# Three passes on split halves for two products of the second block, and square roots by ScalarE from PSUM

## The chip, the cores and the metric

The kernel runs on one core of a Trainium2 chip. The metric is the device time of one execution in microseconds. TensorE (PE) multiplies, VectorE (DVE) and ScalarE (ACT) do elementwise work, GpSimd (POOL) a little, and SyncE (SP) issues nearly all transfers.

## The reference, cut to what matters

A network of three blocks on 256 tokens of width 1024, in fp32. The change lies in the second block, a mixer with two branches. Cut to the lines that matter:

```
h = rmsnorm(x) @ w_in
lru_x, lru_gate, q, k, v, qi, ki, wi, gate_a, gate_b = split(h)
ua = conv(lru_x)
r, i = sigmoid(ua @ wa + ba), sigmoid(ua @ wx + bx)      # blocks of 128
ya = (lru_scan(r, i, ua) * gelu(lru_gate)) @ w_lru_br
qh, kh = rmsnorm(q per head), rmsnorm(k per head)         # q * rsqrt(mean(q*q) + EPS) * q_norm
yb = attention(qh, kh, v, top-k by qi, ki, wi) @ w_attn_br
merged = sigmoid(gate_a) * ya + sigmoid(gate_b) * yb
x = x + merged @ w_out
```

The feed-forward part of the second block follows at once, then the third block.

## The kernel before

Every engine has its own program, written out by hand in the order in which the stages run; semaphores order them against each other. There is no planner: the order in the code is the order of each queue. `make_plan` only counts. It numbers the batches of products (`products_done`), gives each batch of kind "W" one of four work banks in rotation (`bank[4]` to `bank[7]`), and each weight slab one of `NSLOT` = 3 ring slots. `open_bank` makes PE wait until the batch four "W" earlier in the rotation has been read (`bank_copied`). SP loads slab n as soon as the last batch that reads slab n - 3 is done; a slab is 2 MB in two transfers of 1 MB.

A product of activations and weights comes in two forms. The plain one (`feature_major`, `to_acc`) takes the fp32 tiles as they are, one matmul for each 128 rows of the contraction; the trace shows each such matmul as two records. The split one (`feature_major3`, `to_acc3`, both by way of `mm3`) writes each factor as a high half, rounded to fp32r, and a low half, the rest, and makes three matmuls: high by high, high by low, low by high. For this ACT copies a slab's high half into a split area (`high`, two pieces of 128x2048), and DVE subtracts it to get the low half (`low`, two pieces); PE waits for `low_ready`.

The stages of the second block that the prediction speaks of, in PE's order:

- `qk_ms`: five products with `ones_mean` (L1256) give the mean squares of q and k, 128x512 each. DVE adds `EPS` (L2542), which frees the bank, and takes the reciprocal (L2544) in `msq`, two buffers in turn; ACT takes the square root (`rsq`, L1848); DVE multiplies it onto q or k (L2546).
- `qi`: a split product, 96 matmuls on two work banks.
- `lru_ri`: eight batches of plain matmuls (L1265), copied out by ACT with a sigmoid (L1853). On ACT the square roots of `qk_ms` stand between the copies of `qi` and these sigmoids.
- `kiwi`, `gate_a`, the indexer with `gate_b`, `logits2`, `lru_out`: plain products. Beside them DVE runs the LRU's scan, the top-k and the softmax.
- `pv2`: for four pairs of heads m, six transposes (L1321 to L1323) into two banks, ACT's two copies to `pT2`, then four matmuls with v (L1333, L1334) and ACT's copy to `o2`.
- `attn_out` (two slabs, 64 plain matmuls, L954), then on DVE a product with a gate and a sum into `merged` for each of its four batches (L2640, L2645); `w_out2` (two slabs, 32 plain matmuls of 512 columns, L1002) adds to the accumulators.
- `norm3` (L922) and the feed-forward, in split form from the start.

```
        for m in range(4):
            for d in range(2):
                b = open_bank("pv2", 3 * m + d)
                batch(causal_blocks(b, lambda t: att[t][:, 2 * m + d, :]))
...
        all_copied("pv2", (2, 5, 8, 11))
        for s in range(2):
            feature_major("attn_out", 2 * s, s, o2, DC)
        pe.wait_ge(S["merged_ready"], 4)
        for s in range(2):
            to_acc("w_out2", s, merged)
```

Of the kernel before, what the change touches and what calls it, by code (L numbers as in the profile page):

```python
# [31 lines left out]
T, D = 256, 1024  # L32
# [168 lines left out]
def make_plan():  # L201
# [94 lines left out]
def network(nc, dram, out, const_at, col_at, row_at):  # L296
# [189 lines left out]
    xn_flat = xn[:, :, :].rearrange("p t d -> p (t d)")  # L486
    w_o_areas = [[AB[:, 0:2048], AB[:, 2048:4096]] if len(split_areas(f"w_o{h}", 0)) == 1 else [xn_flat, A[8][:, :]]
                 for h in range(2)]
# [111 lines left out]
    def wide(a, dim, n):  # L600
# [8 lines left out]
             "xn_ready", "conv_ready", "z_ready", "logit_ready", "exp_ready", "prob_ready", "mask_ready",  # L609
             "zeroed", "msq_ready", "sel_ready", "sel_prob_ready", "xe_ready", "w_scaled", "slots_ready", "e_y_ready", "rows_out", "bias_in",  # L610
             "lam_exp_in", "lam_exp_out", "sp_ready", "ua_ready", "tanh_done", "decay_done", "mult_in",
             "mult_out", "scan_done", "lru_ready", "rsq_ready", "qk_ready", "relu_used", "att_in", "att_exp",
             "att_ready", "merged_ready", "conv_in", "gelu_done", "rope_ready", "final_row_in", "high_ready",
             "low_ready", "high_norm", "h0_split", "y_high", "o_high", "hid_whole", "hid_split", "cmp_x_ready", "cmp_in",
# [5 lines left out]
             "ffnorm2", "swa_norm", "ffnorm3", "final"]  # L620
    N_INPUTS, N_FILLS = 16 * 9, 5
    R_NORMS = [2, 4, 6, 7, 8, 9, 10, 11]
# [234 lines left out]
    def _(pe):  # L857
# [138 lines left out]

        def to_acc(name, s, src):

            w = slab(name, s)
            for t in range(TT):  # L1000
                for k in range(DC):
                    last = mm(acc[t][s][:, :], src[:, k, t * P:(t + 1) * P], w[:, 512 * k:512 * k + 512],  # L1002
                              start=(k == 0), stop=(k == DC - 1))
            batch(last)

        pe.wait_ge(fills_done, N_FILLS)
# [312 lines left out]
        def causal_blocks(b, p_of_t):  # L1319
# [3 lines left out]
            return nc.tensor.transpose(b[:, 2 * P:3 * P], p_of_t(1)[:, P:2 * P], ident)  # L1323

        for m in range(4):
            for d in range(2):
                b = open_bank("pv2", 3 * m + d)
                batch(causal_blocks(b, lambda t: att[t][:, 2 * m + d, :]))
            b = open_bank("pv2", 3 * m + 2)
            g = m // 2  # L1330
            for d in range(2):
                copied(pe, "pv2", 3 * m + d)
                mm(b[:, d * T:(d + 1) * T], v2[:, 0, g * P:(g + 1) * P], pT2[d][:, 0:T], start=True, stop=False)  # L1333
                last = mm(b[:, d * T + P:(d + 1) * T], v2[:, 1, g * P:(g + 1) * P], pT2[d][:, T:T + P],  # L1334
                          start=False, stop=True)
# [325 lines left out]
    def _(act):  # L1661
# [38 lines left out]
        def high(name, s, it=0):  # L1700

            j = split_number(name, s) - 1
            if plan.times[name] == 1 and j >= 2 and not name.startswith("ffn"):
# [152 lines left out]
        for i in range(2):  # L1856
            rsq(2 * i)
            if i == 0:
                rsq(1)
            copy_out("qi", i, qi[:, 2 * i:2 * i + 2, :].rearrange("p g t -> p (g t)"))  # L1860
        ri(0)
        rsq(3)
        for i in range(1, 5):
            ri(i)
        rsq(4)
        for i in range(5, 8):
            ri(i)
# [34 lines left out]
        for t in range(TT):  # L1902
# [4 lines left out]
            ins.then_inc(S["att_exp"], 1)  # L1907
        for m in range(4):
            for d in range(2):
                copy_out("pv2", 3 * m + d, pT2[d][:, 0:384], n=384)  # L1910
            copy_out("pv2", 3 * m + 2, o2[:, 2 * m:2 * m + 2, :].rearrange("p g t -> p (g t)"))
        filled(act, "attn_out", 3)
# [176 lines left out]
    def _(pool):  # L2089
        pool.dma_start(cols[:, :], dram("cols")).then_inc(cols_loaded, 16)  # L2090
        fills = [(c_pad[:, :, :], 0.0), (ones[:, :], 1.0), (ones_mean[:, :], 1.0 / P), (zeros[:, :], 0.0),
                 (neg_half[:, :], -0.5)]
        assert len(fills) == N_FILLS
# [48 lines left out]
    def _(dve):  # L2142
# [396 lines left out]
        for i in range(5):  # L2539
            a, r = (q2[:, 2 * i:2 * i + 2, :] if i < 4 else k2[:, :, :]).rearrange("p c t -> p (c t)"), msq[i % 2]  # L2540
# [93 lines left out]
        for i in range(1, 4):  # L2634
            gated_lru(i)
        for i in range(4):
            copied(dve, "gate_b", GATE_B_AT[i])
# [5 lines left out]
            copied(dve, "lru_out", i)  # L2643
            a = merged[:, two, :].rearrange("p c t -> p (c t)")
            v.tensor_tensor(a, a, tmp[i % 2][:, :], ALU.add).then_inc(S["merged_ready"], 1)  # L2645
        low("ffn2_first", 0)
# [359 lines left out]
```

## Time and profile before

| | |
|---|---|
| time before, median of 3 runs | 2821.01 us (2817.1 to 2821.4) |
| the profiled execution's own time | 2818.57 us |
| its span | 2816.7 us |
| PE busy | 2463.9 us, 87% of the span |
| DVE busy | 1266.4 us, 45% |
| ACT busy | 776.6 us, 28% |
| `qk_ms` to `kiwi` on PE | 1314.7 to 1350.0 us |
| `pv2` to the end of `w_out2` on PE | 1453.9 to 1522.8 us |

The profile is one execution. Each engine's share is an average over the whole program; what a stage is limited by is read in its own stretch of time. "Idle before" beside an instruction says how long its engine had nothing to do, and which instruction let it go on. PEclk is the granted clock of TensorE as a share of 2.4 GHz; 0.50 is the lower of its two levels, 1.2 GHz. A matmul's listed duration includes its pipeline; the pace of a stream of matmuls is the distance of their starts.

### The profile page before, as it was taken

The numbers are of one execution on the slowest core, as the hardware profiler recorded it, in microseconds if no ns is written. First come the engines' busy times: TensorE is split into PE (matmuls) and PEld (weight loads), VectorE is DVE, ScalarE is ACT, GpSimd is POOL, SyncE is SP. The second block draws the span as 40 slices with busy tenths as digits, with TensorE's granted clock in tenths as the row PEclk, the third lists the DMA queues.
The fourth block names the chain that finished last, engine by engine and source line by source line (L and its number), as shares of the span: only waits on it lengthen the run. The fifth ranks groups of instructions, "written<-read, shape, count | busy, mean of one in ns | idle before, by whom it ended". The sixth has DMA issues, their size and how long they took to land.

```text
span 2816.7 us, 35438 instructions
## 1 busy us (share of the span) xinstructions
PE 2463.9 (87%) x14525; PEld 1712.4 (61%) x14526; DVE 1266.4 (45%) x1841; ACT 776.6 (28%) x1102; POOL 22.3 (1%) x39
## 2 busy tenths in 40 slices
PE   6999877677677766789999999999989999997998
PEld 4997222121122212158787998888958888885887
DVE  2365100000000000046544776876576778776676
ACT  3342000000000000034422334434264434345432
POOL 1000000000000000000000000000000000000000
PEclk9999876777776777799999999999999999998999
DMA  8667999999999999984434554554404555551553
GB/s 319 227 238 305 407 416 416 418 418 419 418 417 417 418 419 418 418 310 139 152 120 150 183 193 170 178 187 166 152 27 150 179 181 192 183 175 61 180 179 120
DMA packets 272134, 720.74 MB, mean 256 GB/s; under 512 B 11240, under 2 KB 129016, under 8 KB 238880
## 3 DMA queue, kind: packets, MB, share of 16 engines
q1 hardware_dynamic: 270000, 708.88, 66.5%
q0 software_dynamic: 2032, 10.40, 1.0%
q8 instruction: 76, 1.25, 0.2%
q14 instruction: 26, 0.21, 0.0%
HBM read 718.17 MB, written 3.16 MB: 256 GB/s over the span
## 4 chain that ended last, share of the span: by engine, by line
PE 52%; issue 41%; DVE 3%; DMA 2%; ACT 2%; POOL 0%; SPq 0%; DVEq 0%; POOLq 0%; ACTq 0%
PE bank L1363 9%; PE bank L887 6%; PE bank L888 6%; PE bank L889 6%; PE bank L1364 4%; PE bank L954 4%; PE bank_pair L887 4%; PE bank_pair L888 3%; PE bank_pair L889 3%; DVE ring_r L2169 1%; PE bank_pair L1002 1%; DMA ring<-in_w_in 1%; PE bank L1014 1%; DVE HT L2797 0%; PE bank_pair L1529 0%
## 5 line engine op out<-in xcount | busy, mean ns | idle before, releaser
L1364 PE MATMUL bank<-HT_r,ring_r 128*128 128x256 f32 x1408 | 395.1, 281 | 0.0
L2428 DVE TENSOR_TENSOR A<-bank,A 128x512 f32<-128x512 f32 x16 | 11.1, 691 | 582.3 <-PE bank L1163 582.3
L1364 PEld LDWEIGHTS bank<-HT_r,ring_r 128*128 128x128 f32 x1408 | 266.2, 189 | 0.7
L889 PE MATMUL bank<-HT_r,ring_r 128*128 128x256 f32 x904 | 255.7, 283 | 0.0
L1363 PE MATMUL bank<-HT_r,AB_r 128*128 128x512 f32 x640 | 228.4, 400 | 1.5 <-DVE HT_r L2177 1.5
L1363 PE MATMUL bank<-HT_r,AC_r 128*128 128x512 f32 x640 | 226.5, 398 | 0.0
L2169 DVE TENSOR_TENSOR ring_r<-ring,AB_r 128x2048 fp32r<-128x2048 f32 (+1 forms) x80 | 177.5, 2260 | 101.2 <-ACT AB_r L1707 101.2
L1163 PE MATMUL bank<-ring,A 128*32 128x512 f32 x768 | 141.3, 825 | 77.6 <-DMA ring<-in_w_gate_e 43.4
L2169 DVE TENSOR_TENSOR ring_r<-ring,A_r 128x2048 fp32r<-128x2048 f32 (+1 forms) x89 | 191.8, 2190 | 21.8 <-ACT A_r L1707 21.8
L2169 DVE TENSOR_TENSOR ring_r<-ring,AC_r 128x2048 fp32r<-128x2048 f32 x66 | 148.5, 2289 | 74.9 <-ACT AC_r L1707 74.7
L889 PE MATMUL bank_pair<-A_r 128*128 128x512 f32 x456 | 178.7, 392 | 0.0
L1707 ACT ACTIVATE AB_r<-ring 128x2048 fp32r<-128x2048 f32 (+1 forms) x80 | 146.7, 1883 | 108.2 <-DMA ring<-in_w_up 36.5
L888 PE MATMUL bank_pair<-ring_r,A_r 128*128 128x512 f32 x448 | 174.5, 390 | 0.0
L889 PEld LDWEIGHTS bank<-HT_r,ring_r 128*128 128x128 f32 x904 | 173.4, 192 | 0.0
L1919 ACT ACTIVATE tmp<-tmp 128x256 f32<-128x256 f32 x112 | 46.8, 418 | 436.4 <-DVE tmp L2690 321.0
L1707 ACT ACTIVATE A_r<-ring 128x2048 fp32r<-128x2048 f32 (+1 forms) x89 | 158.9, 1827 | 3.2 <-PE bank L954 3.2
L1667 ACT ACTIVATE A<-bank 128x256 f32<-128x256 f32 (+1 forms) x69 | 30.1, 447 | 450.9 <-PE bank L1170 302.3
L887 PE MATMUL bank_pair<-A_r 128*128 128x512 f32 x384 | 149.7, 390 | 0.0
L2210 DVE TENSOR_REDUCE tmp<-bank 128x256 f32<-128x512 f32 x176 | 120.7, 686 | 63.3 <-PE bank L1364 63.2
L1707 ACT ACTIVATE AC_r<-ring 128x2048 fp32r<-128x2048 f32 x66 | 123.2, 1916 | 88.2 <-DMA ring<-in_ffn_w_gu 78.1
L1795 ACT ACTIVATE A<-bank 128x512 f32<-128x512 f32 x16 | 9.6, 597 | 497.8 <-PE bank L1163 497.8
L1363 PEld LDWEIGHTS bank<-HT_r,AB_r 128*128 128x128 f32 x640 | 120.6, 189 | 31.4 <-issue 2.1
(502 smaller groups left out, 4614.9 us busy)
## 6 DMA issues: line engine op xcount, KB each, us to landing
ring<-in_ffn_w_gu SPq DMA_DIRECT2D x88, 1024.0 KB, 7.5
ring<-in_w_up_e SPq DMA_DIRECT2D x48, 1024.0 KB, 26.6
ring<-in_w_gate_e SPq DMA_DIRECT2D x48, 1024.0 KB, 22.8
ring<-in_w_down_e SPq DMA_DIRECT2D x48, 1024.0 KB, 19.5
ring<-in_w_in SPq DMA_DIRECT2D x46, 1024.0 KB, 7.3
ring<-in_ffn_w_down SPq DMA_DIRECT2D x40, 1024.0 KB, 6.5
A<-in_w_gate_e SPq DMA_DIRECT2D x32, 1024.0 KB, 19.0
A<-in_w_up_e SPq DMA_DIRECT2D x32, 1024.0 KB, 26.7
```

Source lines behind the costliest of these rows:

```text
L887: mm(out_, lhs[0], rhs[0], start=start, stop=False, skip_group_check=True)
L888: mm(out_, lhs[0], rhs[1], start=False, stop=False, skip_group_check=True)
L889: return mm(out_, lhs[1], rhs[0], start=False, stop=stop, skip_group_check=True)
L954: last = mm(b[:, f * T:(f + 1) * T], w[:, at:at + P], src[:, k, :], start=(k == 0), stop=(k == n_k - 1))
L1163: last = mm(b[32 * j:32 * j + 32, :], xe_now[:, k, :], w[:, 512 * j:512 * j + 512], start=(k == 0), stop=(k == DC - 1), tile_position=(0, ...
L1363: mm(both, high, h_both[:, :, k, :], start=(k == 0), stop=False, skip_group_check=True)
L1364: last = mm(both[:, 1, :], low, h_high[:, k, :], start=False, stop=(k == DC - 1), skip_group_check=True)
L1667: frees(run(dst, work_bank(name, i)[0:rows_, 0:n], ACT.Copy, scale=scale), name, i)
L1707: run(area[:, :], w[:, at:at + area.shape[1]], ACT.Copy).then_inc(S["high_ready"], 1)
L1919: run(f_act[b % 2], f_conv[b % 2], fn).then_inc(S["gelu_done"], 1)
L2169: v.tensor_tensor(twins[f"ring{slot}"][:, part], ring[slot][:, part], area[:, :].bitcast(fp32), ALU.subtract).then_inc(S["low_ready"], 1)
L2210: frees(v.tensor_reduce(dst, both, AX.X, ALU.add), name, i)
```

## The change

In the `qk_ms` stage ACT reads the mean squares straight from PSUM, adds `EPS` as the activation's bias (a new column `eps_col`, filled by POOL at the start) and writes the root to one of five buffers `root` (four in `xn`, one in `tmp[2]`); DVE takes the reciprocal there. All five roots stand ahead of the copies of `qi` on ACT.

`attn_out` and `w_out2` become split products. Their slabs are split by ACT and DVE (`high`, `low`), `o2` and `merged` are written as high and low halves, PE turns the next pair of heads in `pv2` before it multiplies the present one (`pT2` has four buffers now), and it starts `w_out2` without waiting for all four parts of `merged`.

```diff
+def pv2_at(m, part, d=0):
+    if part == "out":
+        return 3 * m + 4 if m < 3 else 11
+    return d if m == 0 else 3 * m - 1 + d
...
-    p.add("attn_out", "WWWW", [1, 3])
-    p.add("w_out2", "AA", [0, 1])
+    p.add("attn_out", "WWWW", [1, 3], split=2)
+    p.add("w_out2", "AA", [0, 1], split=2)
...
-        for m in range(4):
+        pv2_turned(0)
         for m in range(4):
-            for d in range(2):
-                b = open_bank("pv2", 3 * m + d)
-                batch(causal_blocks(b, lambda t: att[t][:, 2 * m + d, :]))
-            b = open_bank("pv2", 3 * m + 2)
+            if m < 3:
+                pv2_turned(m + 1)
+            b = open_bank("pv2", pv2_at(m, "out"))
...
-        all_copied("pv2", (2, 5, 8, 11))
+        def o2_fresh(k):
+            if k % 2 == 0:
+                copied(pe, "pv2", pv2_at(k // 2, "out"))
+            return o2_parts(k)
         for s in range(2):
-            feature_major("attn_out", 2 * s, s, o2, DC)
-        pe.wait_ge(S["merged_ready"], 4)
-        for s in range(2):
-            to_acc("w_out2", s, merged)
+            feature_major3("attn_out", 2 * s, s, o2_parts if s else o2_fresh, src=o2_parts)
+        def pair_merged(k):
+            if k % 2 == 0:
+                pe.wait_ge(S["merged_ready"], k // 2 + 1)
+        to_acc3("w_out2", 0, merged_high, merged_low, ready=pair_merged)
+        to_acc3("w_out2", 1, merged_high, merged_low)
...
# ScalarE
-        def rsq(i):
-            act.wait_ge(S["msq_ready"], i + 1)
-            run(msq[i % 2][:, :], msq[i % 2][:, :], ACT.Sqrt).then_inc(S["rsq_ready"], 1)
+        for i in range(5):
+            filled(act, "qk_ms", i)
+            frees(run(root[i][:, :], work_bank("qk_ms", i)[:, :], ACT.Sqrt, bias=eps_col[:, 0:1]), "qk_ms", i)
...
+        copied(act, "logits2", 7)
+        for s in range(2):
+            high("attn_out", s)
+        for m in range(5):
+            if m < 4:
+                for d in range(2):
+                    copy_out("pv2", pv2_at(m, "turned", d), pT2[2 * (m % 2) + d][:, 0:384], n=384)
+            if m:
+                two_ = slice(2 * m - 2, 2 * m)
+                filled(act, "pv2", pv2_at(m - 1, "out"))
+                run(o2_high[:, two_, :].rearrange("p g t -> p (g t)"),
+                    work_bank("pv2", pv2_at(m - 1, "out"))[:, :], ACT.Copy).then_inc(S["o2_high"], 1)
+        for s in range(2):
+            high("w_out2", s)
...
# VectorE
-            filled(dve, "qk_ms", i)
-            frees(v.tensor_scalar(r[:, :], work_bank("qk_ms", i)[:, :], EPS, None, ALU.add), "qk_ms", i)
             copied(dve, "qk_ms", i)
-            v.reciprocal(r[:, :], r[:, :]).then_inc(S["msq_ready"], 1)
-            dve.wait_ge(S["rsq_ready"], i + 1)
+            link(v.reciprocal(r[:, :], r[:, :]))
...
         for i in range(1, 4):
             gated_lru(i)
+            if i < 3:
+                low("attn_out", i - 1)
+        for m in range(4):
+            i, two = pv2_at(m, "out"), slice(2 * m, 2 * m + 2)
+            dve.wait_ge(S["o2_high"], m + 1)
+            frees(v.tensor_tensor(o2_low[:, two, :].rearrange("p g t -> p (g t)"), work_bank("pv2", i)[:, :],
+                                  o2_high[:, two, :].rearrange("p g t -> p (g t)").bitcast(fp32), ALU.subtract),
+                  "pv2", i)
+        low("w_out2", 0)
...
-            v.tensor_tensor(a, a, tmp[i % 2][:, :], ALU.add).then_inc(S["merged_ready"], 1)
+            v.tensor_tensor(a_high, a, tmp[i % 2][:, :], ALU.add)
+            v.tensor_tensor(a, a, tmp[i % 2][:, :], ALU.add).then_inc(S["merged_whole"], 1)
+            dve.wait_ge(S["merged_whole"], i + 1)
+            v.tensor_tensor(a_low, a, a_high.bitcast(fp32), ALU.subtract).then_inc(S["merged_ready"], 1)
+        low("w_out2", 1)
         low("ffn2_first", 0)
```

ScalarE's queue from the copy of v to the sigmoids of `lru_ri`, before (L1667 copies a batch of `qi`; L1848 is the root, L1853 the sigmoid; the first row is the copy of v):

```order
L1667 ACTIVATE A<-bank 128x512
L1848 ACT_TABLE_LOAD
L1848 ACTIVATE tmp<-tmp 128x512 x2
L1667 ACTIVATE A<-bank 128x512
L1848 ACTIVATE tmp<-tmp 128x512
L1667 ACTIVATE A<-bank 128x512
L1853 ACT_TABLE_LOAD
L1853 ACTIVATE AC<-bank,cols 128x256 x2
L1848 ACT_TABLE_LOAD
L1848 ACTIVATE tmp<-tmp 128x512
L1853 ACT_TABLE_LOAD
L1853 ACTIVATE AC<-bank,cols 128x256 x6
```

The same place on ScalarE in the changed kernel (L1873 is the root, L1692 the copy, L1878 the sigmoid):

```order
L1692 ACTIVATE A<-bank 128x512
L1873 ACT_TABLE_LOAD
L1873 ACTIVATE xn<-bank,eps_col 128x512 x4
L1873 ACTIVATE tmp<-bank,eps_col 128x512
L1692 ACTIVATE A<-bank 128x512 x2
L1878 ACT_TABLE_LOAD
L1878 ACTIVATE AC<-bank,cols 128x256 x8
L1878 ACTIVATE A<-bank,cols 128x256 x8
```

The five roots now read the banks and stand in one row under one table load; the sigmoids are no longer interrupted.

TensorE's queue in `pv2`, before (L1321 to L1323 transpose a head, L1333 and L1334 multiply with v; `tmp2`, `tmp3` hold the turned heads):

```order
L1321 MATMUL bank7<-consts,A4 128x128
L1322 MATMUL bank7<-consts,A8 128x128
L1323 MATMUL bank7<-consts,A8 128x128
L1333 MATMUL bank4<-tmp2,A5 128x256
L1334 MATMUL bank4<-tmp2,A5 128x128
L1333 MATMUL bank4<-tmp3,A5 128x256
L1334 MATMUL bank4<-tmp3,A5 128x128
L1321 MATMUL bank5<-consts,A4 128x128
```

The same place on TensorE in the changed kernel (L1327 to L1329 transpose, L1346 and L1347 multiply):

```order
L1327 MATMUL bank7<-consts,A4 128x128
L1328 MATMUL bank7<-consts,A8 128x128
L1329 MATMUL bank7<-consts,A8 128x128
L1327 MATMUL bank4<-consts,A4 128x128
L1328 MATMUL bank4<-consts,A8 128x128
L1329 MATMUL bank4<-consts,A8 128x128
L1327 MATMUL bank5<-consts,A4 128x128
L1328 MATMUL bank5<-consts,A8 128x128
L1329 MATMUL bank5<-consts,A8 128x128
L1346 MATMUL bank6<-tmp2,A5 128x256
L1347 MATMUL bank6<-tmp2,A5 128x128
```

The six transposes of the next pair now stand between a pair's transposes and its product.

VectorE's queue from the second gated part of `lru_out` (L2649) to the first split of `w_out2` in the changed kernel (L2196 is `low`, L2666 the low half of `o2`); before, only the three rows of L2649 (there L2624) stood here, without the others:

```order
L2649 TENSOR_TENSOR A<-bank,AC 128x512
L2196 TENSOR_TENSOR ring_r<-ring,AB_r 128x2048 x2
L2649 TENSOR_TENSOR A<-bank,AC 128x512
L2196 TENSOR_TENSOR ring_r<-ring,xn_r 128x2048
L2196 TENSOR_TENSOR ring_r<-ring,HT_r 128x2048
L2649 TENSOR_TENSOR A<-bank,AC 128x512
L2666 TENSOR_TENSOR HT_r<-bank,AC_r 128x512 x4
L2196 TENSOR_TENSOR ring_r<-ring,A_r 128x2048 x2
```

The splitting of both slabs of `attn_out` stands between the gated parts of `lru_out`.

## Rows read from the trace of the kernel before

**Rows 1.** The page: the chain that ended last, by engine.
```profile
PE 52%; issue 41%; DVE 3%; DMA 2%; ACT 2%; POOL 0%; SPq 0%; DVEq 0%; POOLq 0%; ACTq 0%
```

**Rows 2.** Stretches: length, busy of PE, PEld, DVE, ACT, POOL, PEclk, DMA.
```profile
1322.00:1326.00 4.00, 3.99 (x21) 4.00 (x22) 3.30 (x2) 0.63 (x1) 0.00 (x0) 0.57 0.00 0
1454.00:1466.00 12.00, 9.14 (x58) 7.74 (x57) 0.69 (x1) 5.55 (x12) 0.00 (x0) 1.00 0.49 175
```

**Rows 3.** Timeline of PE from `qk_ms` to `kiwi`.
```profile
1318.11 1.02 PE L1256 MATMUL bank<-tmp,ones_mean 128*128 128x512 f32 x2
1322.01 0.36 PE L887 MATMUL bank<-AB_r,AC_r 128*128 128x256 f32 x1 [2.88 <-DVE tmp L2542]
...
1325.13 0.41 PE L887 MATMUL bank<-AB_r,A_r 128*128 128x256 f32 x1
...
1328.01 0.28 PE L888 MATMUL bank<-AB_r,A_r 128*128 128x256 f32 x1
1328.13 0.28 PE L889 MATMUL bank<-AB_r,ring_r 128*128 128x256 f32 x1
...
1335.09 1.03 PE L1265 MATMUL bank<-AC,ring 128*128 128x256 f32 x4
1341.42 8.64 PE L1265 MATMUL bank<-AC,ring 128*128 128x256 f32 x28 [5.30 <-DVE tmp L2542]
1349.99 6.31 PE L1270 MATMUL bank<-HT,w_kiwi 128*64 128x256 f32 x32
```

**Rows 4.** Timeline of ACT, then of DVE, in and behind that stretch.
```profile
1315.49 1.28 ACT L1848 ACT_TABLE_LOAD   x1
...
1337.20 0.84 ACT L1853 ACTIVATE AC<-bank,cols 128x256 f32<-128x256 f32 x2
...
1321.90 3.35 DVE L2544 RECIPROCAL tmp<-tmp 128x512 f32<-128x512 f32 x1
...
1390.40 0.28 DVE L2577 TENSOR_SCALAR A<-A,small 128x128 f32<-128x128 f32 x1 [5.30 <-ACT A L1894]
```

**Rows 5.** Timeline from `pv2` to `w_out2`.
```profile
1453.92 0.27 PE L1321 MATMUL bank<-consts,A 128*128 128x128 f32 x1
...
1454.47 0.27 PE L1323 MATMUL bank<-consts,A 128*128 128x128 f32 x1
...
1455.09 0.67 PE L1333 MATMUL bank<-tmp,A 128*128 128x256 f32 x2 [0.34 <-ACT tmp L1667]
...
1456.47 0.27 PE L1321 MATMUL bank<-consts,A 128*128 128x128 f32 x1
...
1465.75 27.86 PE L954 MATMUL bank<-AC,ring 128*128 128x256 f32 x128 [0.99 <-ACT AC L1667]
...
1495.19 27.73 PE L1002 MATMUL bank_pair<-ring,A 128*128 128x512 f32 x64 [1.58 <-DVE A L2645]
```

**Rows 6.** Timeline of PE in `swa_out`, a split product of the third block.
```profile
2595.18 0.77 PE L887 MATMUL bank_pair<-A_r,HT_r 128*128 128x512 f32 x1 [4.59 <-DVE A_r L2893]
...
2597.87 0.63 PE L887 MATMUL bank_pair<-A_r,HT_r 128*128 128x512 f32 x1
2598.30 0.63 PE L888 MATMUL bank_pair<-ring_r,HT_r 128*128 128x512 f32 x1
...
2599.03 0.39 PE L887 MATMUL bank_pair<-A_r,HT_r 128*128 128x512 f32 x1
...
2601.79 0.39 PE L887 MATMUL bank_pair<-A_r,HT_r 128*128 128x512 f32 x1
```

**Rows 7.** Splitting a slab on ACT and DVE; a slab's issue and landing.
```profile
1501.91 3.71 ACT L1707 ACTIVATE AB_r<-ring 128x2048 fp32r<-128x2048 f32 x2 [36.52 <-DMA ring<-in_w_up]
1503.85 4.49 DVE L2169 TENSOR_TENSOR ring_r<-ring,AB_r 128x2048 fp32r<-128x2048 f32 x2 [8.71 <-ACT AB_r L1707]
...
1440.31 0.92 SPq L698 DMA_DIRECT2D ring<-in_w_attn_br  x2
...
ring<-in_w_attn_br SPq DMA_DIRECT2D x2, 1024.0 KB, 6.1
```

More of the change, by code:

```diff
@@ L350, in network @@
     neg_half = sb("neg_half", [P, 2 * TT])
+    eps_col = sb("eps_col", [P, 1])
     tmp = [sb(f"tmp{i}", [P, 512]) for i in range(4)]
@@ L468, in split_areas @@
             return [(0, t_["A3"]), (2048, twins["xn"][:, :, :].rearrange("p t d -> p (t d)"))]
+        if name == "attn_out":
+            xn_r = twins["xn"][:, :, :].rearrange("p t d -> p (t d)")
+            return [(0, t_["AB"])] if s == 0 else [(0, xn_r), (2048, twins["HT"][:, 2048:4096])]
+        if name == "w_out2":
+            a, b = (("A4", "A8"), ("A5", "A6"))[s]
+            return [(0, t_[a]), (2048, t_[b])]
         if name == "swa_kv":
@@ L486, in network @@
     xn_flat = xn[:, :, :].rearrange("p t d -> p (t d)")
+    root = [xn_flat[:, 512 * i:512 * i + 512] for i in range(4)] + [tmp[2]]
     w_o_areas = [[AB[:, 0:2048], AB[:, 2048:4096]] if len(split_areas(f"w_o{h}", 0)) == 1 else [xn_flat, A[8][:, :]]
@@ L995, in to_acc3 @@
             batch(last)
[L997 to L1004, printed above, removed]
         pe.wait_ge(fills_done, N_FILLS)
@@ L1323, in causal_blocks, with pv2_turned, o2_parts @@
             return nc.tensor.transpose(b[:, 2 * P:3 * P], p_of_t(1)[:, P:2 * P], ident)
+        def pv2_turned(m):
+            for d in range(2):
+                b = open_bank("pv2", pv2_at(m, "turned", d))
+                batch(causal_blocks(b, lambda t: att[t][:, 2 * m + d, :]))
+        pv2_turned(0)
         for m in range(4):
-            for d in range(2):
-                b = open_bank("pv2", 3 * m + d)
-                batch(causal_blocks(b, lambda t: att[t][:, 2 * m + d, :]))
-            b = open_bank("pv2", 3 * m + 2)
+            if m < 3:
+                pv2_turned(m + 1)
+            b = open_bank("pv2", pv2_at(m, "out"))
             g = m // 2
             for d in range(2):
-                copied(pe, "pv2", 3 * m + d)
-                mm(b[:, d * T:(d + 1) * T], v2[:, 0, g * P:(g + 1) * P], pT2[d][:, 0:T], start=True, stop=False)
-                last = mm(b[:, d * T + P:(d + 1) * T], v2[:, 1, g * P:(g + 1) * P], pT2[d][:, T:T + P],
+                copied(pe, "pv2", pv2_at(m, "turned", d))
+                p = pT2[2 * (m % 2) + d]
+                mm(b[:, d * T:(d + 1) * T], v2[:, 0, g * P:(g + 1) * P], p[:, 0:T], start=True, stop=False)
+                last = mm(b[:, d * T + P:(d + 1) * T], v2[:, 1, g * P:(g + 1) * P], p[:, T:T + P],
                           start=False, stop=True)
             batch(last)
-        all_copied("pv2", (2, 5, 8, 11))
-        for s in range(2):
-            feature_major("attn_out", 2 * s, s, o2, DC)
-        pe.wait_ge(S["merged_ready"], 4)
-        for s in range(2):
-            to_acc("w_out2", s, merged)
+        def o2_parts(k):
+            return o2_high[:, k, :], o2_low[:, k, :]
+        def o2_fresh(k):
+            if k % 2 == 0:
+                copied(pe, "pv2", pv2_at(k // 2, "out"))
+            return o2_parts(k)
+        for s in range(2):
+            feature_major3("attn_out", 2 * s, s, o2_parts if s else o2_fresh, src=o2_parts)
[4 more added lines that the diff above has]
+        to_acc3("w_out2", 1, merged_high, merged_low)
         def gate_up_tile(name, i, w, j, it=0, parts=h_parts):
@@ L1702, in high @@
             j = split_number(name, s) - 1
-            if plan.times[name] == 1 and j >= 2 and not name.startswith("ffn"):
+            if plan.times[name] == 1 and j >= 2 and not name.startswith("ffn") \
+                    and name not in ("attn_out", "w_out2"):
                 act.wait_ge(products_done, plan.split_end[j - 2])
@@ L1856, in _ @@
         for i in range(2):
-            rsq(2 * i)
-            if i == 0:
-                rsq(1)
             copy_out("qi", i, qi[:, 2 * i:2 * i + 2, :].rearrange("p g t -> p (g t)"))
[L1861 to L1866, printed above, removed]
+        for i in range(8):
             ri(i)
@@ L1907, in _ @@
             ins.then_inc(S["att_exp"], 1)
-        for m in range(4):
-            for d in range(2):
-                copy_out("pv2", 3 * m + d, pT2[d][:, 0:384], n=384)
-            copy_out("pv2", 3 * m + 2, o2[:, 2 * m:2 * m + 2, :].rearrange("p g t -> p (g t)"))
+        copied(act, "logits2", 7)
[3 more added lines that the diff above has]
+            if m < 4:
+                for d in range(2):
+                    copy_out("pv2", pv2_at(m, "turned", d), pT2[2 * (m % 2) + d][:, 0:384], n=384)
[6 more added lines that the diff above has]
+            high("w_out2", s)
         filled(act, "attn_out", 3)
@@ L2539, in _ @@
         for i in range(5):
-            a, r = (q2[:, 2 * i:2 * i + 2, :] if i < 4 else k2[:, :, :]).rearrange("p c t -> p (c t)"), msq[i % 2]
-            filled(dve, "qk_ms", i)
-            frees(v.tensor_scalar(r[:, :], work_bank("qk_ms", i)[:, :], EPS, None, ALU.add), "qk_ms", i)
+            a = (q2[:, 2 * i:2 * i + 2, :] if i < 4 else k2[:, :, :]).rearrange("p c t -> p (c t)")
+            r = root[i]
             copied(dve, "qk_ms", i)
-            v.reciprocal(r[:, :], r[:, :]).then_inc(S["msq_ready"], 1)
-            dve.wait_ge(S["rsq_ready"], i + 1)
+            link(v.reciprocal(r[:, :], r[:, :]))
             v.scalar_tensor_tensor(a, a, col("q_norm_2" if i < 4 else "k_norm_2"), r[:, :], ALU.mult, ALU.mult)\
@@ L2643, in _ @@
             copied(dve, "lru_out", i)
-            a = merged[:, two, :].rearrange("p c t -> p (c t)")
-            v.tensor_tensor(a, a, tmp[i % 2][:, :], ALU.add).then_inc(S["merged_ready"], 1)
+            a, a_high, a_low = (m_[:, two, :].rearrange("p c t -> p (c t)")
+                                for m_ in (merged, merged_high, merged_low))
+            v.tensor_tensor(a_high, a, tmp[i % 2][:, :], ALU.add)
[3 more added lines that the diff above has]
+        low("w_out2", 1)
         low("ffn2_first", 0)
```

16 lines of the change are left out of this document (8 added, 8 removed).

## The prediction

> **What bounds the kernel now.** I read the page's chain first: PE holds 52% of it and PE's own issue 41%, DVE, DMA and ACT 7% together [rows 1]. The expert stage apart, where transfers limit, the program is as long as PE's stream of matmuls plus the holes in it. So I looked for holes around the two places that the change touches, in the timeline of PE.
>
> In the first place there are two. PE finishes the last mean square at 1319.1 (1318.11 + 1.02) and starts `qi` at 1322.01, after 2.88 us of idle time; it does one batch of `lru_ri` at 1335.09 and sits idle for 5.30 us until 1341.42. Both rows name DVE's L2542, which frees a bank that the next batch needs [rows 3]. DVE frees one bank per round of add, reciprocal (3.35 us), ACT's root and product [rows 4]. The clock shows too: PEclk is 0.57 from 1322 to 1326 [rows 2], and the matmuls there start 0.208 us apart (1322.01 to 1325.13, fifteen matmuls), against 0.12 later [rows 3].
>
> In the second place, `pv2` goes in rounds: six transposes, a wait for ACT's copy, four matmuls with v, a wait for the next. Only 9.14 of 12 us are busy, with PEclk 1.00 [rows 2]. Then `attn_out` takes 27.86 us for 128 records (64 matmuls), 1.58 us pass until `merged` is whole, and `w_out2` takes 27.73 us for 64 records (32 matmuls) [rows 5]. These two run without a hole: there the matmuls themselves are the limit.
>
> **The change part by part.** The sum is made against the profiled execution's own 2818.57 us, 2.4 below the median of 2821.01. Times below are on the clock of the trace before.
>
> *Roots.* ACT's table load ends at 1316.77 [rows 4]. A root of 128x512 from PSUM is not in the trace before; I take it as some 0.6 us, since two sigmoids of half the size take 0.84 [rows 4]; even at 0.84 nothing changes below. The bank of the second mean square, which `qi` needs first, is then free at about 1318, before PE is through the fifth product at 1319.1. `qi` starts at 1319.1, not 1322.01. Its 96 matmuls need 96 x 0.12 = 11.5 us and end at 1330.6, not 1335.09: 4.5 us gained, 2.9 of it idle time and 1.6 low clock.
>
> `lru_ri` is 4 + 28 = 32 records [rows 3]. At the pace of `attn_out`, 27.86 / 128 = 0.218 us [rows 5], they take 7.0 us. The stage ends at 1337.6, where `kiwi` starts; before, `kiwi` started at 1349.99 [rows 3]. Is ACT fast enough? It copies the last batch of `qi` after 1330.6 (0.6 us), loads a table (1.28), then needs 0.86 per batch [rows 4]: the first is done near 1333.4, when PE, four banks ahead, asks for it at 1334.1. It keeps step. **Gain 12.4 us** (1349.99 - 1337.6). If `lru_ri` still ran at low clock as it did in part before (28 records in 8.64 us, 2.5 more than at 0.218), it is 9.9.
>
> DVE must come as much earlier, or PE meets it later. Its five rounds lose the add and the wait for the root, and end near 1338; its next work waits for ACT's last sigmoid, near 1339.5. Before, that sigmoid could not end before the last batch of `lru_ri`, at 1350.0. So DVE goes on at least 10.5 us earlier, against PE's 12.4, and it was idle for 5.30 us before the first score [rows 4], which covers the rest. The stages from `kiwi` to `lru_out` move as a whole.
>
> *pv2.* A transpose is 0.11 us (1453.92 to 1454.47, five steps), a round's product 1.38 (1455.09 to 1456.47) [rows 5]. With the next pair's transposes ahead of the product, ACT's copies lie beside them. 24 x 0.11 + 4 x 1.38 = 8.2 us instead of 11.83 (1453.92 to 1465.75): **3.6 us gained**. The bank of a turned pair is freed by ACT's copy one round earlier, that of a product by DVE's low half. The last low half comes some 1.9 us after the last product; `attn_out` needs it only at its seventh k, 6 x 0.36 = 2.2 us in. That cover is thin; without it it costs tenths.
>
> *attn_out.* 64 plain matmuls become 192 split ones at 0.12 us [rows 3], the same 256 columns: 23.0 instead of 27.86 us, **4.8 gained**.
>
> *Between.* DVE now makes four passes of 0.7 us for the last part of `merged`, 2.9 us. But `w_out2` starts with parts 0 to 2 and meets part 3 after 6 x 0.69 = 4.1 us. **1.5 us gained** (the 1.58). If this cover failed, about as much is lost again.
>
> *w_out2.* 32 matmuls become 96. In `swa_out` the same shape starts every 0.23 us (2599.03 to 2601.79, twelve) [rows 6]: 22.1 instead of 27.73, **5.6 gained**.
>
> Here a rule can be set beside the rows, outside of the sum. The Trainium skill (FP8 and Floating Point Precision, TensorE Precision Notes) says that true FP32 takes four passes through the array. By its page TensorE: Matmul & The Clock Gate (Back-to-back issue gap) a pass takes N / 2.4 + 2.5 ns, 109 ns for 256 columns and 216 for 512. The plain pace here (0.218 for one of two records) agrees with four such passes. The split pace (0.12 and 0.23) is slower than the rule. By the rule the two products would take 20.9 and 20.7 us, 3.5 less than my sum. No run here shows it; the rows decide.
>
> *Splitting.* A slab costs ACT 3.71 and DVE 4.49 us, DVE starting 1.94 behind ACT [rows 7]; four new slabs. For `attn_out`'s second slab the transfers are issued at 1440.31 and land after 6.1 us, so near 1447.3; ACT splits until 1451.0, DVE until 1453.8, just before the first transposes end. Behind ACT's splitting stand the copies of `pv2`, wanted at 1454.4: 3.4 us to spare. Behind DVE's stands the last gated part of `lru_out`, which frees the bank for the fourth turned head: a few tenths to spare. `w_out2`'s first slab is split while `attn_out` runs. Its second is loaded when `attn_out`'s first slab is used up (1473.6), split by ACT until about 1485, by DVE behind the last part of `merged`, 1488 to 1492.5. PE wants it when the first half of `w_out2` ends, near 1496. `ffn2_first`'s first slab is issued when `attn_out` ends, as before, and wanted a full `w_out2` later. All of this costs nothing while these covers hold. The one more fill on POOL at the start lies under the first transfers.
>
> Sum: 12.4 + 3.6 + 4.8 + 1.5 + 5.6 = 27.9 us. 2818.57 - 27.9 = 2790.7; I say 2791.
>
> **The rivals.**
> (a) *The splitting comes late.* DVE or ACT is behind at one of the thin places, PE waits some microseconds and falls to the low clock. `swa_out` shows the pattern: 4.59 us idle for a low half, then matmuls 0.43 apart until 2598.7 (eight, 1.6 us lost) [rows 6]. One such wait costs 6.2 us: 2797. Against it: the slack above.
> (b) *The hole of the roots is met again.* If DVE's chain to the scores did not come forward, PE would get its 12.4 us but hand back all beyond DVE's 5.30 us of slack, 7.1: 2798. Against it: DVE's own earlier start.
> (c) *A split matmul takes half a plain record.* A plain record of 256 columns starts every 0.218 us, one of 512 every 27.73 / 64 = 0.433 [rows 5]. If each is two passes and a split matmul one, 192 x 0.109 + 96 x 0.217 = 41.8 us stand against my 45.1, 3.3 less: 2787. Against it: split matmuls start 0.12 and 0.23 us apart [rows 3, 6]. The rule of four passes, in the Trainium skill (FP8 and Floating Point Precision, TensorE Precision Notes), would make it so.
> (d) *Slower than before.* The split products run at low clock throughout. Then they start 0.208 and 0.43 us apart: 192 x 0.208 + 96 x 0.43 = 81.2 us instead of 45.1, and the time is 2827. It decides once 77% of them (27.9 of 36.1) run low. For it: PE falls after every long hole. Against it: PEclk is 1.00 even in `pv2` with its holes [rows 2].
> (e) *The change does not do what it says*, the roots or the products wait for something not seen, and nothing is gained: 2819.
>
> **How the numbers follow.** The full sum 0.72, (a) 0.13, (b) 0.05, (c) 0.04, (d) 0.03, (e) 0.03. The likeliest case has a range of its own of 2787 to 2795: `pv2` between its sum and 1 us more, the low clock in `lru_ri` 2.5 more, a slack that fails by tenths. To leave out no more than 2 in 10 I take (c) in and (a) and (b) nearly: 2786 to 2799. Faster by over 0.2% (5.6 us, about what a measurement tells from no change) hold all but (d) and (e): 0.94; same 0.03; slower 0.03.
>
> **What would show it.** Right: no idle time of PE over 1 us from the mean squares to `kiwi`, `kiwi` 12 us earlier, one table load for the roots and one for the sigmoids; 192 matmuls in 23 us and 96 in 22; the first `norm3` transpose 28 us earlier. Wrong: an idle row of PE in `pv2`, at the start of `attn_out` or between the halves of `w_out2` with DVE's or ACT's splitting as its releaser, PEclk under 0.9 from `pv2` to `w_out2`, or a longer wait for the scores.

## The result, and the profile after

| | before | changed |
|---|---|---|
| median of 4 runs each | 2821.19 us (2817.1 to 2821.4) | 2790.85 us (2787.4 to 2793.43) |
| ratio, with its 95% interval | | 0.9895 (0.9878 to 0.9912) |
| the profiled execution's span | 2816.7 us | 2791.6 us |

The kernel became faster by 30.3 us, 1.05%; the interval of the ratio leaves out 1. A second set of runs of the two gave 2818.07 and 2789.74 us, ratio 0.9902 (0.9885 to 0.9918). The prediction was 2791, with a range of 2786 to 2799.

The page's chain of the changed kernel reads as before, answering to [rows 1]: the program is still PE's stream and its issue.

```profile
PE 53%; issue 41%; DVE 3%; ACT 1%; DMA 1%; POOL 0%; DVEq 0%; SPq 0%; POOLq 0%; ACTq 0%
```

The timeline of PE in the changed kernel, from the first mean square to `gate_a`, answers to [rows 3] (L1262 the mean squares, L902 to L904 the split matmuls, L1271 `lru_ri`, L1276 and L1282 the two batches of `kiwi`, L969 plain matmuls):

```profile
1317.42 3.59 PE L1262 MATMUL bank<-A,ones_mean 128*128 128x512 f32 x8
1320.85 1.02 PE L1262 MATMUL bank<-tmp,ones_mean 128*128 128x512 f32 x2
1321.31 0.68 PE L902 MATMUL bank<-AB_r,AC_r 128*128 128x256 f32 x1
...
1333.22 7.07 PE L1271 MATMUL bank<-AC,ring 128*128 128x256 f32 x32
1340.22 6.32 PE L1276 MATMUL bank<-HT,w_kiwi 128*64 128x256 f32 x32
1346.47 4.65 PE L1282 MATMUL bank<-w_kiwi,HT 128*128 128x8 f32 x32
1350.97 1.63 PE L969 MATMUL bank<-HT,ring 128*128 128x256 f32 x3
```

No row has idle time any more. `qi` follows the last mean square, and the 32 records of `lru_ri` run as one group of 7.07 us. ACT's rows show why, beside [rows 4]: one table load, four roots within 2.42 us, the fifth 0.69.

```profile
1318.23 1.28 ACT L1873 ACT_TABLE_LOAD   x1
1319.53 2.42 ACT L1873 ACTIVATE xn<-bank,eps_col 128x512 f32<-128x512 f32 x4
1321.91 0.69 ACT L1873 ACTIVATE tmp<-bank,eps_col 128x512 f32<-128x512 f32 x1
```

The timeline from `pv2` to the feed-forward in the changed kernel answers to [rows 5]:

```profile
1445.81 0.27 PE L1327 MATMUL bank<-consts,A 128*128 128x128 f32 x1
...
1446.69 0.27 PE L1329 MATMUL bank<-consts,A 128*128 128x128 f32 x1
1447.09 0.33 PE L1327 MATMUL bank<-consts,A 128*128 128x128 f32 x1
...
1453.95 0.36 PE L902 MATMUL bank<-AC_r,AB_r 128*128 128x256 f32 x1
...
1477.07 0.40 PE L902 MATMUL bank_pair<-A_r,AC_r 128*128 128x512 f32 x1
...
1498.86 2.20 PE L937 MATMUL bank<-consts,x 128*128 128x128 f32 x16
1501.57 0.36 PE L902 MATMUL bank<-HT_r,AB_r 128*128 128x256 f32 x1 [0.50 <-DVE HT_r L2204]
```

`pv2` takes 8.14 us (1445.81 to 1453.95), `attn_out` 23.12, `w_out2` 21.79, and nothing lies between them. The starts from 1446.69 to 1447.09 are 0.40 us apart where transposes otherwise start every 0.11: a small hole of 0.3 us. Over both products PE is busy throughout and PEclk is 1.00 (length, PE busy, PEclk, share and rate of the transfers):

```profile
1454.00:1498.00 44.00, 44.00 (x287) 1.00 0.44 144
```

To compare kernels I take stretches of PE's timeline, from the start of one stage's first matmul to the next's, since these hardly vary, while the time at which the first mean square starts does (1313.3 to 1317.6 us over the profiles of this study, whose code up to there is nearly the same: the expert stage, bound by transfers, varies).

| stretch, us | before | changed | roots_only | products_only |
|---|---|---|---|---|
| first mean square to `kiwi` | 35.31 | 22.80 | 22.80 | 35.26 |
| second batch of `kiwi` to the indexer | 33.08 | 34.74 | 34.74 | 33.08 |
| `pv2` | 11.83 | 8.14 | 11.83 | 8.04 |
| `attn_out`, with the gap behind it | 29.44 | 23.12 | 29.44 | 23.12 |
| `w_out2` | 27.58 | 21.79 | 27.58 | 21.79 |
| first mean square to the feed-forward | 210.79 | 184.15 | 199.94 | 194.85 |

The stretches that the table leaves out, up to the feed-forward, are the same in all four within 0.01 us: `kiwi`'s first batch 6.25, the indexer to `pv2` 64.6, `norm3` 2.70.

The profiled spans differ by 25.1 us. The stretches of the last line differ by 26.64. The changed execution came 2.74 us later to the first mean square (1317.42 against 1314.68), and its part behind the feed-forward's start was 1.20 us shorter (1290.03 against 1291.23). Both lie outside of the changed code.

### The profile page after: what moved, and what is told of

It reads as the page before. It is cut to its first block, busy times and chain, and to the rows that moved or that the text cites. A ratio compares the mean times of both kernels' runs of the same rounds, so it can differ in the third digit from the quotient of the medians.

```text
span 2791.6 us, 35652 instructions
## 1 busy us (share of the span) xinstructions
PE 2459.9 (88%) x14622; PEld 1722.5 (62%) x14622; DVE 1289.0 (46%) x1856; ACT 785.5 (28%) x1106; POOL 22.4 (1%) x40
## 3 DMA queue, kind: packets, MB, share of 16 engines
q8 instruction: 76, 1.25, 0.2%
## 4 chain that ended last, share of the span: by engine, by line
PE 53%; issue 41%; DVE 3%; ACT 1%; DMA 1%; POOL 0%; DVEq 0%; SPq 0%; POOLq 0%; ACTq 0%
PE bank L1388 9%; PE bank L902 6%; PE bank L903 6%; PE bank L904 6%; PE bank L1389 4%; PE bank_pair L902 4%; PE bank_pair L903 4%; PE bank_pair L904 4%; PE bank L969 3%; DVE ring_r L2196 1%; PE bank L1020 1%; DVE HT L2836 0%; PE bank L1492 0%; PE bank L1508 0%; DVE small L2824 0%
## 5 line engine op out<-in xcount | busy, mean ns | idle before, releaser
L904 PE MATMUL bank<-HT_r,ring_r 128*128 128x256 f32 x904 | 256.1, 283 | 0.0
L2196 DVE TENSOR_TENSOR ring_r<-ring,AB_r 128x2048 fp32r<-128x2048 f32 (+1 forms) x82 | 182.0, 2261 | 96.5 <-ACT AB_r L1733 96.5
L1169 PE MATMUL bank<-ring,A 128*32 128x512 f32 x768 | 147.1, 857 | 77.0 <-DMA ring<-in_w_gate_e 42.7
L2196 DVE TENSOR_TENSOR ring_r<-ring,A_r 128x2048 fp32r<-128x2048 f32 (+1 forms) x93 | 200.8, 2194 | 22.8 <-ACT A_r L1733 22.8
L904 PE MATMUL bank_pair<-A_r 128*128 128x512 f32 x488 | 191.6, 393 | 0.0
L2196 DVE TENSOR_TENSOR ring_r<-ring,AC_r 128x2048 fp32r<-128x2048 f32 x66 | 148.5, 2289 | 72.7 <-ACT AC_r L1733 72.6
L904 PEld LDWEIGHTS bank<-HT_r,ring_r 128*128 128x128 f32 x904 | 173.8, 192 | 0.0
L1733 ACT ACTIVATE A_r<-ring 128x2048 fp32r<-128x2048 f32 (+1 forms) x93 | 166.4, 1830 | 19.5 <-DMA ring<-in_w_out 16.3
L1692 ACT ACTIVATE A<-bank 128x256 f32<-128x256 f32 (+1 forms) x69 | 30.4, 450 | 458.7 <-PE bank L1176 303.6
L902 PE MATMUL bank_pair<-A_r 128*128 128x512 f32 x384 | 149.7, 390 | 0.0
L903 PE MATMUL bank<-HT_r,AB_r 128*128 128x256 f32 x504 | 143.0, 284 | 0.0
## 6 DMA issues: line engine op xcount, KB each, us to landing
ring<-in_w_up_e SPq DMA_DIRECT2D x48, 1024.0 KB, 26.6
A<-in_w_up_e SPq DMA_DIRECT2D x32, 1024.0 KB, 26.6
```

The costliest lines, as they stand in the source:

```text
L902: mm(out_, lhs[0], rhs[0], start=start, stop=False, skip_group_check=True)
L903: mm(out_, lhs[0], rhs[1], start=False, stop=False, skip_group_check=True)
L904: return mm(out_, lhs[1], rhs[0], start=False, stop=stop, skip_group_check=True)
L1169: last = mm(b[32 * j:32 * j + 32, :], xe_now[:, k, :], w[:, 512 * j:512 * j + 512], start=(k == 0), stop=(k == DC - 1), tile_position=(0, ...
L1692: frees(run(dst, work_bank(name, i)[0:rows_, 0:n], ACT.Copy, scale=scale), name, i)
L2196: v.tensor_tensor(twins[f"ring{slot}"][:, part], ring[slot][:, part], area[:, :].bitcast(fp32), ALU.subtract).then_inc(S["low_ready"], 1)
```

## The experiments

**roots_only** is the kernel before with the roots' part alone.

```diff
+        for i in range(5):
+            filled(act, "qk_ms", i)
+            frees(run(root[i][:, :], work_bank("qk_ms", i)[:, :], ACT.Sqrt, bias=eps_col[:, 0:1]), "qk_ms", i)
...
-            frees(v.tensor_scalar(r[:, :], work_bank("qk_ms", i)[:, :], EPS, None, ALU.add), "qk_ms", i)
```

> The kernel before with the roots' part alone. Theory (two separate gains): from the first mean square to kiwi 22.8 us, as in the changed kernel (22.80), against 35.31 before; from pv2 to norm3 68.9 us as before; time 12 us (less what is handed back behind kiwi, about 1.7) under the kernel before, so 0.9955 to 0.9965 of it. Rival (the parts help each other, the roots alone only move the wait): the stretch shortens, but PE waits later, at the scores or at lru_out, and the time falls by 7 us or less.

Measured: 2805.9 us against 2819.44, ratio 0.9950 (0.9934 to 0.9967). The stretch is 22.80 us, the rest as in the table: 10.85 us gained up to the feed-forward. The stretches came as the theory says and the rival is out; the time fell by 13.5 us, a little more than forecast, and the interval reaches into the forecast. The 1.66 us handed back behind `kiwi` appear here too, without the split products. The roots' part changes several things at once: ACT frees the bank in its first step, the roots have five buffers instead of two, and they stand ahead of the copies of `qi` under one table load. Which of them counts was not tested.

**products_only** is the changed kernel with the roots made as before.

```diff
+            rsq(2 * i)
+            if i == 0:
+                rsq(1)
             copy_out("qi", i, qi[:, 2 * i:2 * i + 2, :].rearrange("p g t -> p (g t)"))
```

> The changed kernel with the roots made as before (DVE adds, ACT roots a copy). Theory: first mean square to kiwi 35.3 us as before; pv2 to norm3 53.1 us as in the changed kernel (53.05, before 68.85); time about 16 us under the kernel before, 0.994 to 0.995 of it. Rival (the splitting on ACT and DVE only fits because the roots' part moved DVE forward): PE waits in pv2 or attn_out and the stretch is 55 us or more.

Measured: 2801.8 us against 2819.44, ratio 0.9937 (0.9920 to 0.9953), again a little more than forecast. From `pv2` to `norm3` 52.95 us, with no idle row. The splitting fits without the roots' part. By stretches the two parts alone give 10.85 + 15.94 = 26.79 us, together 26.64: they add up.

The next four kernels (merged_wait, dve_late, pv2_rounds, four_passes) ran once each, with 2793.91, 2792.55, 2793.31 and 2805.01 us. A single time moves by several us with the expert stage, so only their stretches are read.

**merged_wait** takes the cover away that hides the last part of `merged`.

```diff
+        pe.wait_ge(S["merged_ready"], 4)
         to_acc3("w_out2", 0, merged_high, merged_low, ready=pair_merged)
```

> The changed kernel, but PE waits for all four parts of merged before it starts w_out2. Theory (the cover of 4.1 us hides DVE's four passes of 0.7 us): PE idle for 2.9 to 3.1 us between attn_out and w_out2, then matmuls 0.43 us apart for 2 to 4 us, so that w_out2's stretch grows by 1 to 2 us as well: attn_out's end to norm3 26 to 27 us instead of 21.8. Rival (DVE's last part is done at once, the gap before was only the semaphores' way): 22 to 23.5 us.

The timeline of PE in merged_wait, at the start of `w_out2`:

```profile
1477.67 0.50 PE L902 MATMUL bank_pair<-A_r,AC_r 128*128 128x512 f32 x1 [2.91 <-DVE A_r L2684]
1478.00 0.39 PE L903 MATMUL bank_pair<-ring_r,AC_r 128*128 128x512 f32 x1
...
1479.49 0.63 PE L902 MATMUL bank_pair<-A_r,AC_r 128*128 128x512 f32 x1
1479.91 0.63 PE L903 MATMUL bank_pair<-ring_r,AC_r 128*128 128x512 f32 x1
```

PE waits 2.91 us, and a little later the starts are 0.42 us apart. The stretch from `attn_out` to `w_out2` is 26.19 us (3.07 more), `w_out2` itself 23.49 (1.70 more): together from the end of `attn_out` to `norm3` 26.6 us, as the theory says. Waiting part by part is worth 4.77 us here, and over a third of it is the clock (PEclk is 0.50 from 1479 to 1482).

**dve_late** gives DVE 4.6 us more work ahead of the last gated part of `lru_out`.

```diff
+            if i == 3:
+                for _ in range(2):
+                    link(v.tensor_tensor(A[6][:, :], A[6][:, :], A[6][:, :], ALU.max))
             gated_lru(i)
```

> The changed kernel with two passes of DVE over 128x2048 (2.3 us each, results used by nothing) ahead of the last gated part of lru_out. Theory (DVE's cover there is used up, the changed kernel's PE already waits 0.3 us for that bank): PE waits 4.6 us more in pv2, after which the clock falls for some 3 to 4 us; pv2 8.1 to 13 us, and attn_out's start runs at the low clock if the fall outlasts pv2: pv2 to the end of attn_out 31.3 to 36.5-38 us. Rival (PE has slack there that the trace does not show): under 33 us.

The timeline of dve_late in `pv2`, DVE and PE:

```profile
1442.09 4.61 DVE L2662 TENSOR_TENSOR A<-A 128x2048 f32<-128x2048 f32 x2
...
1446.74 0.69 DVE L2649 TENSOR_TENSOR A<-bank,AC 128x512 f32<-128x512 f32 x1
...
1447.49 0.47 PE L1327 MATMUL bank<-consts,A 128*128 128x128 f32 x1 [4.64 <-DVE A L2649]
1447.76 0.42 PE L1328 MATMUL bank<-consts,A 128*128 128x128 f32 x1
```

The extra passes go over to PE whole. `pv2` takes 14.08 us, 5.94 more, which is past the 13 that the theory gave it; `attn_out` takes its 23.12, 37.20 in sum, within the theory's wide range. The rival, under 33, is out. The clock is back before `attn_out`. This is the prediction's rival (a) made on purpose: 4.6 us of lateness cost 5.9.

**pv2_rounds** keeps the split products, but turns one pair of heads, copies it and multiplies, as before.

```diff
-        return 3 * m + 4 if m < 3 else 11
-    return d if m == 0 else 3 * m - 1 + d
+        return 3 * m + 2
+    return 3 * m + d
...
-        pv2_turned(0)
         for m in range(4):
-            if m < 3:
-                pv2_turned(m + 1)
+            pv2_turned(m)
```

ACT's copies go back into that order too.

> The changed kernel with pv2 in its old rounds (turn a pair, copy, multiply), split products kept. Theory: pv2 takes 11.8 us instead of 8.14, plus up to 0.7 since DVE's low half now frees a bank in each round and stands ahead of attn_out; everything else as in the changed kernel. Rival (the new order gained nothing, the split o2 did): 8 to 9 us.

A row of the timeline of PE in pv2_rounds, the start of a round's product:

```profile
1451.36 0.67 PE L1344 MATMUL bank<-tmp,A 128*128 128x256 f32 x2 [0.50 <-ACT tmp L1690]
```

The waits of 0.50 us are back, but `pv2` takes 10.58 us, less than the theory's 11.8 and more than the rival's 8 to 9: each holds in part. The new order is worth 2.44 us of the 3.69 gained. The other 1.25 come from the start of `attn_out`: it no longer waits for all of ACT's copies, only for the heads of its first k. In pv2_rounds it starts 0.14 us after the last matmul of `pv2` (1455.23 and 1455.37), in the kernel before 1.38 us after it (1464.37 and 1465.75).

**four_passes** adds a fourth matmul, low by low, to each product of `attn_out` and `w_out2`.

```diff
             mm(out_, lhs[0], rhs[0], start=start, stop=False, skip_group_check=True)
+            if fourth[0]:
+                mm(out_, lhs[1], rhs[1], start=False, stop=False, skip_group_check=True)
```

> The changed kernel with a fourth matmul (low by low) for each product of attn_out and w_out2. It computes slightly more than the changed kernel. Theory (a split matmul costs what it costs, 0.12 us for 256 columns and 0.23 for 512, more than half a plain record): attn_out 256 x 0.12 = 30.7 us, w_out2 128 x 0.228 = 29.2 us, both slower than the plain products of the kernel before (27.86 and 27.6). Rival (c of the prediction, a split matmul is half a plain record, the third pass only seemed dear): 27.9 and 27.7 us.

The timeline of PE in four_passes, where `attn_out` begins, where `w_out2` begins and where it ends:

```profile
1451.67 0.36 PE L904 MATMUL bank<-AC_r,AB_r 128*128 128x256 f32 x1
...
1482.47 0.40 PE L904 MATMUL bank_pair<-A_r,AC_r 128*128 128x512 f32 x1
...
1511.52 0.71 PE L941 MATMUL bank<-consts,x 128*128 128x128 f32 x5
```

`attn_out` takes 30.80 us for 256 matmuls, 0.120 each, `w_out2` 29.05 for 128, 0.227 each. Rival (c), half a plain record or 0.109 and 0.217, is out. With four split matmuls both stages are slower than their plain forms of 27.86 and 27.58 us; the gain hangs on leaving the fourth (low by low) away. The Trainium skill (FP8 and Floating Point Precision, TensorE Precision Notes) says that true FP32 takes four passes. If so, 27.86 us over 4 x 64 passes are 0.109 each and 27.58 over 4 x 32 are 0.215, the prediction's own figures by that rule; the trace shows two records for each such matmul, not its passes. A pass counted so costs a tenth less than a split matmul of 256 columns and a twentieth less than one of 512.

**kiwi_woven** goes after the time handed back. The windows of the changed kernel show PEclk from 1349 to 1356 us, where the narrow matmuls of `kiwi` (8 columns) end and `gate_a` begins:

```profile
1349.00:1356.00 7.00, 7.00 (x23) 0.51 0.62 229
```

The clock falls though PE has no idle time. The kernel before has a shorter fall at the same place, PEclk 0.50 from 1360 to 1363. kiwi_woven puts the 16 narrow matmuls one by one between the first 16 of `gate_a`.

```diff
+        for f in range(2):
+            for k in range(DC):
+                narrow_ = mm(b[:, f * 8:(f + 1) * 8], hT[:, k, f * P:(f + 1) * P], w_kiwi[:, k, 64:72],
+                             start=(k == 0), stop=(k == DC - 1), skip_group_check=True)
...
+                last = mm(b_a[:, f * T:(f + 1) * T], w[:, 512 * k + f * P:512 * k + (f + 1) * P], hT[:, k, :],
+                          start=(k == 0), stop=(k == DC - 1), skip_group_check=True)
```

> The changed kernel with the 16 narrow matmuls of kiwi's second batch (8 columns) placed one by one between the first 16 matmuls of gate_a. Theory (the granted clock falls because of the unbroken narrow stretch, 3.6 us before and 4.5 in the changed kernel; that is where 1.66 us were handed back): PEclk stays 1.00, and from kiwi's second batch to the indexer 31.1 us or less instead of 34.74 (changed) and 33.08 (before); time 3 to 3.6 us lower than the changed kernel's. Rival (the clock falls for another reason, at that place in time or because of the transfers that now lie beside it): it falls all the same and the stretch stays at 33 to 35 us.

The same stretch as windows, of the kernel before, of the changed one, of merged_wait and of kiwi_woven (length, PE busy, PEclk, share and rate of the transfers):

```profile
1356.24:1389.32 33.08, 33.08 (x162) 0.95 0.21 74
```
```profile
1346.47:1381.21 34.74, 34.74 (x162) 0.90 0.37 135
```
```profile
1345.70:1378.77 33.07, 33.07 (x161) 0.95 0.40 143
```
```profile
1343.68:1375.07 31.39, 31.39 (x161) 1.00 0.42 150
```

With the matmuls woven in, the clock holds at 1.00 and the stretch takes 31.39 us, 3.35 less than in the changed kernel and 1.69 less than in the kernel before; the theory had asked for 31.1 or less. The transfers beside it are no less. Measured: 2787.6 us against 2819.44, ratio 0.9888 (0.9872 to 0.9905). Breaking up the narrow stretch keeps the clock up, as the theory says. One point of it is the wrong way round: the narrow stretch takes 4.5 us instead of 3.6 because the clock falls inside it, so its greater length is a result of the fall.

**changed_again** and **woven_again** are the changed kernel and kiwi_woven unaltered, together on one chip.

> The changed kernel unaltered, for a tighter interval and a second profile. Theory (the clock's fall behind kiwi differs from execution to execution): the stretch from kiwi's second batch to the indexer is either near 33.1 or near 34.75 us, all other stretches as in the first profile within 0.1 us; time 0.989 to 0.9905 of the kernel before. Rival (the longer fall belongs to this kernel): 34.7 again in this profile, and merged_wait's 33.07 was the exception.

> kiwi_woven unaltered, beside the changed kernel on the same chip. Theory: no fall of the clock behind kiwi, 31.4 us for that stretch again, and a time 1.7 to 3.4 us under the changed kernel's, 0.988 to 0.9895 of the kernel before. Rival (the difference of the first medians, 3.2 us, was the spread of the expert stage): the two medians within 1 us of each other, though the stretch is shorter.

Measured: changed_again 2789.74 us (2789.05 to 2792.32), ratio 0.9902 (0.9885 to 0.9918); woven_again 2787.59 us (2787.12 to 2788.92), ratio 0.9893 (0.9876 to 0.9909). The intervals of the ratios overlap, but all four runs of the woven kernel are under all four of the changed one; the difference of the medians is 2.2 us. It is the fastest version of this study. The stretch behind `kiwi` was 34.75 us in changed_again and 31.40 in woven_again.

The expectations of changed_again could not be told apart by this number, which both allow. Over all profiles: of the seven that have the new roots and no weaving, six show 34.73 to 34.75 us and one, merged_wait, 33.07, though its code is the same up to there; both profiles with the old roots show 33.08. So the longer fall goes with the new roots in most profiles, but not with the code alone: merged_wait has the new roots and the shorter one.

What goes with it in all nine is where the clock falls. The 16 narrow matmuls take 3.60, 3.66 and 3.82 us where the stretch is short (before, products_only, merged_wait): the clock falls at most 0.5 us before they end. They take 4.07 to 4.77 us where it is long: the clock falls 1.0 us or more before they end, and stays low twice as long. What sets the moment of the fall stays open.

## Why the prediction was right

The time was forecast to a microsecond, the sum less exactly than that looks.

- *Roots.* 12.4 us forecast, 12.51 measured. Both holes and both falls of the clock are gone, and ACT keeps step. DVE was to come forward by at least 10.5 us and to live on its slack for the rest; it comes forward by 15.4, more than PE. The rows are DVE's first product behind the roots, before and changed, 39.35 and 23.99 us after the first mean square; then its first score, before which it now sits idle for 9.80 us, against 5.30 in [rows 4]:

```profile
1354.03 2.29 DVE L2552 TENSOR_TENSOR A<-A,AC 128x2048 f32<-128x2048 f32 x1 [2.95 <-ACT A L1853]
```
```profile
1341.41 2.29 DVE L2577 TENSOR_TENSOR A<-A,AC 128x2048 f32<-128x2048 f32 x1 [0.82 <-ACT A L1878]
...
1382.29 0.29 DVE L2602 TENSOR_SCALAR A<-A,small 128x128 f32<-128x128 f32 x1 [9.80 <-ACT A L1911]
```

  This rules out rival (b), and PE's stretch from the indexer to `pv2`, 64.6 us in both, agrees. The prediction lists "a longer wait for the scores" as a sign of being wrong; said of DVE, that sign was badly chosen, since DVE waits longer because it is early.

- *The stages from `kiwi` to `lru_out` move as a whole.* This sentence was wrong by 1.66 us, the longer fall of the clock behind `kiwi`. [Rows 3] ended at `kiwi`'s first batch, and I did not look at the granted clock behind its second, where 1.7 us were already lost before the change.
- *pv2.* 3.6 forecast, 3.69 measured. The working put it all down to the transposes; pv2_rounds shows that a third is the earlier start of `attn_out`. Two small errors cancel: a round's product takes 1.31 us and not 1.38 (1447.48 to 1448.79), and the hole of 0.3 us was not in the sum.
- *attn_out.* 4.8 forecast, 4.74 measured.
- *Between.* 1.5 forecast, 1.58 measured. The price set on a failed cover, "about as much is lost again", is right for the waiting: in merged_wait the gap grows by 3.07 us, the 1.58 gained and 1.49 more. It leaves out the clock, which costs another 1.70.
- *w_out2.* 5.6 forecast, 5.79 measured; the pace was 0.227 us, not 0.23.
- *Splitting.* The splits took on ACT and DVE what was worked out, 3.7 and 4.5 us a slab, but that of `attn_out`'s second slab ended 0.7 to 0.8 us later than forecast, measured from the start of `pv2`. Two rows of the changed kernel's timeline show the thin place, the end of DVE's splitting of `attn_out`'s second slab and the gated part behind it:

```profile
1444.15 2.28 DVE L2196 TENSOR_TENSOR ring_r<-ring,HT_r 128x2048 fp32r<-128x2048 f32 x1
1446.35 0.68 DVE L2649 TENSOR_TENSOR A<-bank,AC 128x512 f32<-128x512 f32 x1
```

  The "few tenths to spare" were a few tenths too little: the gated part ends at 1447.03, and the transposes that need its bank go on at 1447.09. That is the hole in `pv2`. Rival (a) did not come about, and dve_late shows that a wait of that length costs about what it was priced at, 5.9 us against 6.2. Rival (c) is out, the matmuls start 0.120 and 0.227 us apart. Rival (d) is out, PEclk is 1.00 over both products; so is (e).

In sum 27.9 us were forecast. The five parts came to 28.3, and less the 1.66 handed back 26.64 were measured up to the feed-forward. The medians differ by 30.3 and, in the second set, by 28.3 us. The 2 to 4 us beyond the stretches lie outside of the changed code, and executions of one kernel differ by as much (2787.4 to 2793.43 us for the changed one). The forecast started from one execution of 2818.57 us, 2.6 under the median that the result is set against. The mechanism was right in its main parts; that the median met the forecast to a microsecond is luck.

## What to carry to other kernels

When a stage holds TensorE up because a bank is freed late, count the lost clock with the idle time: an idle stretch of 2.9 us cost 1.6 to 1.7 us more behind it, both in [rows 3] and in merged_wait. It does not grow evenly with the wait: 1.3 us more behind 4.64 us in dve_late, 2.5 behind the 5.30 of [rows 3]. Where an engine frees a bank late, look for one that can read it in its first step, and put its work under one table load; here both came together. Three split matmuls beat a plain fp32 one by 17 to 21% when the splitting lies beside other work; with four they are 5 to 11% slower, so work the pace out for the shape at hand.

## What the runs showed of the hardware that was not expected

The granted clock fell in a stretch in which TensorE was never idle. While 16 matmuls of 8 columns ran back to back, it went from 1.00 to 0.50. In the changed kernel it fell at 1349.1 and stayed low until 1355.9, far into wide matmuls; in the kernel before it fell as they ended and stayed low half as long. With the same matmuls placed one by one between wide ones it stayed at 1.00, and the stretch went from 34.74 (before: 33.08) to 31.39 us. A timeline without idle time does not say that the clock is up; PEclk has to be read beside it.

The first matmuls after a wait may still run fast: in merged_wait the first five starts lie 0.23 to 0.33 us apart after the 2.91 us of waiting, before the pace drops to 0.43. They need not: in dve_late, after 4.64 us, the starts are 0.21 us apart from the second transpose on, against 0.11 in the changed kernel.
